# Expert rows of U and V gathered as one 8 KB row into one ring of nine, and sums by diagonals, in a hybrid decoder step

## The reference

```
experts = e1 * PEER_KEYS + e2
g = jax.nn.softmax(vs, axis=-1).astype(xb.dtype)
act = jax.nn.gelu(jnp.einsum('nd,nhkd->nhk', xb, peer_u[experts]), approximate=False)
return jnp.einsum('nhk,nhkd->nd', g * act, peer_v[experts])
```

## Time and profile before

| | |
|---|---|
| runs | 3528.41, 3542.61, 3545.09 us; median 3542.61 us |
| profiled execution | span 3534.4 us from first to last instruction; no other time is listed for it |
| PE busy | 2634.4 us, 75% |
| DVE busy | 2374.2 us, 67% |
| POOL busy | 2393.4 us, 68% |
| ACT busy | 433.3 us, 12% |
| DMA | 1321.7 MB, 374 GB/s over the span |

### The profile page before, as it was taken

One profiled execution on the slowest core, in us unless ns is written; L12 is line 12 of the kernel. 1 busy time (PEld: TensorE's weight loads), 2 busy tenths in 40 slices (PEclk: granted clock), 3 DMA queues, 4 the chain that ended last, 5 costly groups with the idle time before them and its releaser, 6 DMA issues.

```text
span 3534.4 us, 35434 instructions
## 1 busy us (share of the span) xinstructions
PE 2634.4 (75%) x11810; PEld 1284.3 (36%) x11810; DVE 2374.2 (67%) x6243; ACT 433.3 (12%) x980; POOL 2393.4 (68%) x2118
## 2 busy tenths in 40 slices
PE   6658676788867798797766777797877778767656
PEld 5634123553432344362232223463332234313211
DVE  4686667667678786767478765867478766847642
ACT  1101100113101231111001110111001110000000
POOL 0155776667757776657767777657767776677876
PEclk8879779898888989899889888999888999988799
DMA  6478999999999999999999999999999999999999
GB/s 252 169 277 313 367 349 408 352 397 369 366 404 362 380 348 408 407 400 377 380 411 402 388 377 409 395 412 395 381 410 397 396 399 407 397 408 384 322 410 371
DMA packets 372025, 1321.73 MB, mean 374 GB/s; under 512 B 60674, under 2 KB 72130, under 8 KB 351618
## 3 DMA queue, kind: packets, MB, share of 16 engines
q0 software_dynamic: 304128, 1107.43, 81.0%
q1 hardware_dynamic: 67714, 212.03, 15.4%
HBM read 1311.41 MB, written 7.88 MB: 373 GB/s over the span
## 4 chain that ended last, share of the span: by engine, by line
POOL 26%; PE 25%; DMA 22%; DVE 15%; issue 10%; SPq 2%; ACT 1%; DVEq 0%; POOLq 0%; ACTq 0%
POOL v_ring L818 13%; POOL u_ring L805 12%; DMA v_ring<-down_rows,codesT 12%; PE ps L863 8%; PE ps L927 6%; DMA u_ring<-up_rows,codes 6%; DMA wbuf<-weights 4%; DVE u_ring L1775 3%; DVE arena L1745 3%; PE ps L917 2%; PE ps L1127 2%; PE ps L1180 2%; DVE idx L1745 1%; DVE top_c L1745 1%; DVE top_v L1745 1%
## 5 line engine op out<-in xcount | busy, mean ns | idle before, releaser
L863 PE MATMUL ps<-v_ring,Z 128*32 128x512 f32 x4096 | 1324.0, 688 | 606.6 <-DMA v_ring<-down_rows,codesT 479.3
L1775 DVE CUSTOM_DVE_ANT_0 u_ring<-u_ring,xn 128x1024 f32<-128x1024 f32 x1056 | 1260.7, 1219 | 596.0 <-DMA u_ring<-up_rows,codes 595.5
L805 POOL DMA_INDIRECT u_ring<-up_rows,codes x1056 | 1191.4, 1128 | 676.6 <-issue 305.8
L818 POOL DMA_INDIRECT v_ring<-down_rows,codesT x1056 | 1200.8, 1137 | 449.3 <-issue 297.9
L863 PEld LDWEIGHTS ps<-v_ring,Z 128*32 128x32 f32 x4096 | 242.9, 118 | 1404.0 <-DMA v_ring<-down_rows,codesT 836.4
L927 PE MATMUL ps<-wbuf,xT 128*128 128x256 f32 (+2 forms) x1184 | 287.4, 401 | 64.8 <-DMA wbuf<-weights 36.5
L1127 PEld LDWEIGHTS ps<-xT,wbuf 128*128 128x128 f32 x2176 | 269.0, 202 | 160.8 <-issue 106.8
L1127 PE MATMUL ps<-xT,wbuf 128*128 128x128 f32 (+1 forms) x2176 | 292.1, 290 | 38.9 <-DMA wbuf<-weights 38.8
L927 PEld LDWEIGHTS ps<-wbuf,xT 128*128 128x128 f32 (+1 forms) x1184 | 226.8, 198 | 139.8 <-DMA wbuf<-weights 41.1
L1745 DVE MAX8 vals<-arena 128x8 f32<-128x128 f32 (+1 forms) x288 | 69.0, 280 | 113.9 <-ACT arena L1560 113.3
L917 PE MATMUL ps<-wbuf,kT 128*128 128x256 f32 (+1 forms) x480 | 104.7, 371 | 0.0
(11 more groups left out here) (332 smaller groups left out, 2358.2 us busy)
## 6 DMA issues: line engine op xcount, KB each, us to landing
wbuf<-weights SPq DMA_DIRECT2D x142, 1024.0 KB, 8.3
u_ring<-up_rows,codes POOLq DMA_INDIRECT x1056, 8.6
v_ring<-down_rows,codesT POOLq DMA_INDIRECT x1056, 8.8
u_ring<-weights SPq DMA_DIRECT2D x8, 1024.0 KB, 14.7
v_ring<-weights SPq DMA_DIRECT2D x8, 1024.0 KB, 14.9
wbuf<-weights SPq DMA_DIRECT2D x9, 768.0 KB, 7.5
resid<-x_prompt SPq DMA_DIRECT2D x8, 512.0 KB, 7.0
table<-decay_in SPq DMA_DIRECT2D x8, 512.0 KB, 10.3
```

The costliest lines, as they stand in the source:

```text
L805: pool.indirect_dma_start(out=u_ring[:, i % U_RING, :], out_offset=None, in_=up_rows, in_offset=bass.IndirectOffsetOnAxis(ap=codes[:, t % ...
L818: pool.indirect_dma_start(out=v_ring[:, v % V_RING, :], out_offset=None, in_=down_rows, in_offset=bass.IndirectOffsetOnAxis(ap=codesT[:, t ...
L863: mm = pe.matmul(acc[32 * c:32 * c + 32, half, :], (Zs if t == TILES else Z)[:, at:at + GS], v_ring[:, v % V_RING, half * 512:(half + 1) * ...
L1775: dve.tensor_tensor_reduce(u, u, xn[:, t % 2], 1.0, 0.0, ALU.mult, ALU.add, dots[:, k:k + 1]).then_inc(dot_done, 1)
```

## The change

U and V rows are put side by side on the host: `expert_rows` has rows of 2,048 floats, 8 KB. One gather per slot brings both, into `ring` with 9 buffers of 8 KB per partition. POOL issues 1,056 gathers and not 2,112; each waits for the sum of the slot 9 before. Row p of a buffer now holds U and V of an expert of position p, so the weighted sum for a slot is a product with a diagonal matrix: ACT multiplies the gelu of the dot with the gate (a column), then multiplies the identity with this column into `diag` (5 buffers), and PE multiplies `diag` with the V half, 128 x 128 by 512 columns, twice. Gelus come in batches of up to 4 slots, 2 slots behind DVE's dots; PE's sums are 3 slots behind DVE's dots. Transposed numbers, `Z`, `coefs`, `place_p` and `make_coefs` are gone. The gates are now made head by head (an exponential on ACT and two small operations on DVE each) since the first sums of a tile come earlier. `FRONTS` and `PEER` stay; `LAST` is adapted, since sums no longer trail by 32 slots.

```diff
-U_RING, V_RING = 8, 9
+RING, DIAGS = 9, 5
+GELU_LAG, SUM_LAG = 2, 3
...
-        LAST = [9, 9, 5, 3, 3, 3] + [3, 3] * H + [2, 2] + [58]
+        LAST = [5, 5, 5, 4, 4, 4] + [3, 4] * H + [3, 3] + [21 + SUM_LAG]
...
-            for k in range(GS):
-                u_rows(0, k)
-            for t in range(TILES):
-                for g in range(GROUPS):
-                    for j in range(GS):
-                        v_rows(t, g, j)
-                        if g + 1 < GROUPS:
-                            u_rows(t, (g + 1) * GS + j)
-                        else:
-                            u_rows(t + 1, j)
...
+                if i >= RING:
+                    pool.wait_ge(v_done, i - RING + 1)
                 pool.indirect_dma_start(
+                    out=ring[:, i % RING, :], out_offset=None, in_=expert_rows,
                     in_offset=bass.IndirectOffsetOnAxis(ap=codes[:, t % 2, k:k + 1], axis=0),
+                ).then_inc(row_in[i % RING], 16)
...
+                pe.wait_ge(diag_ready, i + 1)
+                for c in range(2):
+                    mm = pe.matmul(acc[0:n, c, :], diag[:, i % DIAGS, 0:n], ring[:, i % RING, D + c * 512:D + (c + 1) * 512],
+                                   start=False, stop=(k == slots_of(t) - 1))
+                mm.then_inc(v_done, 1)
...
+            def gelu(first, end):
...
+                act.wait_ge(dot_done, end)
+                own.wait()
+                own.done(act.activation(dots[:, at], dots[:, at], ACT.Gelu))
+                for i in range(first, end):
+                    make_diag(i)
...
+                own.wait()
+                own.done(act.activation(dots[:, k:k + 1], dots[:, k:k + 1], ACT.Copy, scale=gates[:, t % 2, k:k + 1]))
+                if i >= DIAGS:
+                    act.wait_ge(v_done, i - DIAGS + 1)
+                of, m = (stack, ST) if t == TILES else (ident, P)
+                own.wait()
+                own.raises(act.activation(diag[:, i % DIAGS, 0:m], of[:], ACT.Copy, scale=dots[:, k:k + 1]), diag_ready, i + 1)
...
+            def take_gates(t, h, n):
+                dve.wait_ge(gate_exp, H * t + h + 1)
+                if t >= 2 and h == 0:
+                    dve.wait_ge(v_done, SLOTS * (t - 1))
+                do(dve.reciprocal, gate_s[0:n, h:h + 1], gate_s[0:n, h:h + 1])
```

More of the change, by code:

```diff
@@ L837, in _ @@
+            for i in range(TILES * SLOTS + GS):
+                gather(i)
         @block.tensor
@@ L1332, in _ @@
             sample_rest(slots)
-            for r in range(16):
-                v_round(TILES, 0, r)
+            for k in range(GS):
+                add_row(TILES * SLOTS + k)
         @block.scalar
@@ L1369, in put_y, with gelus_and_sums @@
                 own.wait()
-                own.raises(act.activation(ybuf, acc.rearrange("p a b -> p (a b)"), ACT.Copy), y_ready, t + 1)
-            def groups(done, upto):
-                for at in range(done + 1, upto + 1):
-                    if at % GS == 2 and at > GS:
-                        make_Z(*divmod(at // GS - 1, GROUPS))
-                    if at % GS == 0 and at <= SLOTS * TILES:
-                        gelu(*divmod(at // GS - 1, GROUPS))
-                    if at % SLOTS == GS and at > SLOTS:
-                        put_y(at // SLOTS - 1)
+                own.raises(act.activation(ybuf[0:n], acc[0:n].rearrange("p a b -> p (a b)"), ACT.Copy), y_ready, t + 1)
+            def gelus_and_sums(done, upto):
+                at, end = max(done - GELU_LAG, 0), min(max(upto - GELU_LAG, 0), SLOTS * TILES)
+                while at < end:
+                    to = min(end, at + 4, (at // SLOTS + 1) * SLOTS)
+                    gelu(at, to)
+                    at = to
+                t = (upto - SUM_LAG) // SLOTS - 1
+                if t >= 0 and done - SUM_LAG < (t + 1) * SLOTS:
+                    put_y(t)
             def turned_copy(t, j, n, scale):
@@ L1594, in projected @@
                 slots()
-                gate_exps(t - 1, P)
+                for h in range(HEADS_HERE, H):
+                    gate_exps(t - 1, h, P)
                 for _ in range(3):
@@ L1727, in _ @@
             act.wait_ge(first_in, 32)
-            slots = Pace(groups)
+            slots = Pace(gelus_and_sums)
             for t in range(TILES):
@@ L1732, in _ @@
             sample_rest(slots)
-            gelu(TILES, 0)
-            make_Z(TILES, 0)
+            for k in range(0, GS, 4):
+                gelu(TILES * SLOTS + k, TILES * SLOTS + k + 4)
             put_y(TILES)
@@ L2412, in shape_constants @@
         s_same=same, eye=np.eye(P),
-        place_rows=np.eye(P)[:, [32 * (i % 4) + i // 4 for i in range(P)]],
-        place_new=np.array([[float(i // 32 == n % 4 and i % 32 == n // 4) for i in range(P)] for n in range(ST)]),
+        stack_new=np.tile(np.eye(ST), (4, 1)),
         spread_new=np.tile(np.eye(ST), (1, 4)),
```

249 lines of the change are left out of this document (88 added, 161 removed).

## The result

The changed kernel took 3940.01 us in the median (four runs, 3928.40 to 3944.82), the kernel before beside it 3539.61 us. The ratio is 1.115, with a 95% interval of 1.111 to 1.119. The direction was forecast. The time was not: 3745 was said, with 3900 as the upper end, so it lies 195 us above the forecast and 40 us past the range.

The account below looks back on a forecast made before the run. Gathers were taken to bound the kernel from about 281 us on. Terms 121 + 80 + 40 + 20 - 38 - 20 = +203 us on the 3534 us span, with 8 for the median, gave 3745 us; range 3450 to 3900.

Parts of the forecast that it names:

- Bound of the kernel before: Whole kernel before: no engine is full; from about 281 us on it is bound by its gathers.
- Part 1: Gathers: one 8 KB row per slot in place of two gathers, -38 us, with ends 0 and -74.
- Part 4: First slots: without the trail of 32, V rows start 29 slots earlier where DMA idles, -20 us (0 to -30).
- Part 2: PE's expert sums by diagonals: 1.8 us a slot, PE 3,175 us busy in all; early stretch +121 us.
- The early term: Stretch 281 to 1559 us: PE's work and other waits make 1,399 us against 1,278, +121 us.
- Part 3: New chain from DVE's dot through ACT's gelu, weight and diagonal to PE's sum: +80, +40 and +20 us.
- The head chosen: Late attention, a head of tile 7: 12.7 us against 10.24, +80 us over 8 heads in 4 tiles (+35 to +150).
- The PEER part: PEER part: two calls of ACT's chain per head, 1 us a head for 8 heads in 5 tiles, +40 us.
- The other late calls: The other 18 calls in 4 late tiles: 0.3 us each, +20 us.
- C: Rival: the ring of nine is too short, with 2 buffers left for flight; 3900 to 4100 us, chance 0.12.
- A: Rival: the ring is enough, handshakes hide behind nine buffers and DMA bounds; 3448 to 3520 us, chance 0.18.
- D: Rival: gains and losses cancel over the whole kernel; 3525 to 3620 us, chance 0.15.

Follow-up runs that it names:

- x3_both: Changed kernel with PE multiplying by the identity without waiting for ACT's diagonal, and only the first half of each weighted sum formed: 3447.53 us, 0.975 of the kernel before.
- x1_free_diag: Changed kernel with PE multiplying by the identity without waiting for ACT's diagonal, which ACT still forms; whole sums: 3561.65 us, 1.007 of the kernel before.

## Why the prediction was wrong

**Bound of the kernel before, Part 1 and Part 4: right in kind, low in size.** Gathers bound the late part, and the new rows are faster than was taken. x3_both has -103 us behind the mark where the terms were -38. PE's load is like that of before there (line 820 is busy 1,230 us, line 863 was 1,324), so this is the layout's own. The size of the rate was right: in a piece of x3_both with 12 gathers of 1.049 MB in 30 us it is 418 GB/s, where 421 was reckoned:

```profile
3380.00:3410.00 30.00, 19.67 (x24) 2.00 (x24) 14.84 (x24) 7.54 (x26) 13.34 (x12) 0.66 1.01 418
```

In the whole program the layout gives -90, where -58 was taken and -104 was the sum of the lower ends. Over the some 620 slots behind the mark -103 us is 0.17 us a slot, more than twice the 0.07 that the rate gives. What the rest is, the trail or the handshakes of a second ring, was not told apart.

**Part 2: right.** Back to back four slots take 6.87 us in the kernel after, 1.72 a slot, as the two products of the earlier trace rows said:

```profile
3344.67 7.03 PE L818 MATMUL ps<-ring,diag 128*128 128x512 f32 x16
3351.54 1.67 PE L881 MATMUL ps<-wbuf,xT 128*128 128x256 f32 x7
```

The early term was +121; by x1 less x3 it is +103. In x1_free_diag PE is busy 3158.1 us where 3,175 was said, but that is luck in part: the sums take 1981 us and not 1,901, the other steps 1177 and not 1,274, at a granted clock of 0.94 where it was 0.88. The 2135.8 us of line 818 in the kernel after, 2.02 a slot, are more than the 1.8 taken, but the 1.8 returns when the waits go (1919.8 us for 1,024 slots in x1_free_diag, 1.87): most of the rest comes with the waits, which break the sums into shorter runs, and is no cost of the product.

**Part 3, the chain: the step that failed.** It took the chain's price from one late head, added 60 us for the PEER part and the other calls, and gave the first tiles nothing: 80 + 40 + 20 = 140 us. The runs show 378 us (381 by the profiled spans, 130 before the mark and 251 behind it). Three faults, by what each left out:

- *The early tiles had no term* (+130 us). The text reckoned this stretch from PE's work and its 154 us of other waits, as if a wait for ACT could not arise where PE is the bound. Of the 154 us only a third is left: in 153 to 1660 us PE idles 1507 - 1276 = 231 us, and 183 of them are for diagonals (77 times). One kind of wait went and another came. By stage, 52 of the 130 us lie between attention and PEER part, 32 of these beside the sample's mixing in tile 1, where ACT waits up to 19.4 us for dots; 31 in the projections, 30 in the PEER part and 16 in the attention heads. The table loads of the short heads cost more than these 16, but the rest of it stands in the row of the new layout, since x3_both has them too.
- *The head chosen was a cheap kind* (+52 us). The working was good for a head with four slots and dots in time, 12.7 forecast and 12.8 shown. It was set against a head of 10.24 us where the mean of tile 7 was 11.1, and after the change the mean is 16.3, since in tile 7 other heads have five slots or late dots. Late attention in all takes 395 us without the chain and 527 with it: 132 us where 80 was said. The high end, with dots two late, was +150 and does hold it.
- *The PEER part* was priced at 1 us a head (+60 us). From the first search of a tile to the start of its eighth DVE takes 120.2, 132.9 and 122.2 us before in tiles 4 to 6, and 132.9, 150.9 and 134.2 after; in the sample's own part it is 134.9 and 171.3. By stage the chain costs 41 us in tiles 4 to 6 and 59 us from there to the end, 100 where 40 was said.

The other late calls were right: 34 - 14 = 20 us, and +20 was said. So 130 + 52 + 60 us is, to 1 us, the gap between 140 and the 381 us by spans. The late share is 251 and not the 163 seen from outside, since the late part is also -103 us of layout and +16 of PE's work.

**The rivals.** C, 3900 to 4100 us at a chance of 0.12, named the time but not the place. It said the ring was too short; ring 8 costs 39 us at lag 3, and giving buffers more lag *gained* 292 us (3945.44 to 3653.33). Buffers, of rows or of diagonals, seem to limit only at lag 6. The text held both facts, sums that trail by 3 and calls of 4, and drew from them that two buffers are left for flight; the closer reading was that three of four diagonals are not there when PE comes. A and D fell with the chain: A's 3448 us is what x3_both takes (3447.53), D's range is where x1_free_diag lies (3561.65). The Trainium skill's rule, ScalarE: Activation LUTs, section What ACT_TABLE_LOAD costs, of a drain on top of each load would have made late attention +125 us, closer to the 132 measured, but not for that reason: in the kernel after too the gelu starts 0.03 us behind its load (3297.70 + 1.28, then 3299.01), and taking 241 loads away is worth 79 us, less than their rows.

**The range** broke because the upper bound of the chain term was built from one place (+150 us of late attention) and from 0 to 2 us a head elsewhere, with no upper bound for the first three tiles at all.

**The signs.** Most came as written: PE over 3,050 us busy, a DMA share of 0.85 in the early part, 550 us of PE's waits for diagonals, POOL waiting for PE's sums, 1.72 us for two products. PE's 85% did not come (83%), nor did a late head of 12 to 13 us as the mean of tile 7 (16.3): the two that said the chain was longer than priced.

## What to carry to other kernels

When a change ties a chain of small steps into an engine's order, count how many results that engine asks for in the same call in which they are made, and price the wait at every call of every kind, the early stages too; the mean over all heads is the price, a single head is a sample. The lag between maker and user is a constant to be swept before the idea is judged: here 3, 4, 5 and 6 slots gave 3945, 3741, 3653 and (with smaller gelus) 3710 us, the last step being lost, probably to the buffers that the lag holds. A producer at 38% busy can be the bound of the pieces in which its fixed cost, here two table loads, is spent for one result, as early attention shows: 120 us before, 165 after, 126 without the loads.

## What the runs showed of the hardware

- The kernel before takes two times, by chip: 3537.83 and 3538.05 us in two of the sets of runs, 3697.42 and 3672.17 in two others, with a granted clock of 0.87 to 0.89 in the first and 0.84 to 0.86 in the second. The changed kernel doesn't move with it: 3940.01 us where the kernel before takes 3540, 3945.44 where it takes 3672. Lag 4 ran on two chips of the second kind alone. The kernel before was not profiled where it is slow, so what differs is open.
- Rows of 8 KB are gathered at 418 to 420 GB/s where rows of 4 KB came at 409, and the layout, with half sums and no wait of PE for ACT, was worth 90 us.
- 597 us more of busy PE (2634 to 3232) cost 133 us of time in the old order, where the sums trail the dots by 32 slots; 654 us more (2630 to 3285) cost 257 us (3940.01 less 3683.39) inside a chain with a lag of 3 slots.
- A table load is 1.28 us, with the next instruction 0.03 us behind it (3297.70 + 1.28, then 3299.01), and an ACT operation on 128 x 1 elements takes 0.29 us, near the 0.40 us of one on 128 x 128. In this chain of small steps on ACT their count is most of the price, not their size: the 1,056 smallest were worth 86 us.
